# One attention routine: DVE's copy of transposed probabilities ahead of the newest maximum, transposes ahead of scores where there are three score buffers

## The reference, cut to what matters

```
s = jnp.einsum('bqhd,bkhd->bhqk', q_blk, k).astype(jnp.float32) * scale
p = jax.nn.softmax(s, axis=-1).astype(v.dtype)
return jnp.einsum('bhqk,bkhd->bqhd', p, v)
```

## The kernel before, in words

| prefix | what | key columns | loops x pairs of heads | score buffers |
|---|---|---|---|---|
| am | latent, layer one | 1024 | 2 x 2 | 3 |
| ad | dilated, layer one | 1024 | 2 x 2 | 3 |
| aa | maps, two later layers | 1280 | 2 x 2 | 2 |
| ab | grouped, two later layers | 1280 | 1 x 3 | 2 |
| ac | neighbourhood, two later layers | 256 or 384 near, 256 context | 1 x 3 | 3 |

## Time and profile before

### The profile page before, as it was taken

One profiled execution on the slowest core, in us unless ns is written; L12 is line 12 of the kernel. 1 busy time (PEld: TensorE's weight loads), 2 busy tenths in 40 slices (PEclk: granted clock), 3 DMA queues, 4 the chain that ended last, 5 costly groups with the idle time before them and its releaser, 6 DMA issues. The chain is left out here.

```text
span 4864.1 us, 71195 instructions
## 1 busy us (share of the span) xinstructions
PE 3732.1 (77%) x24823; PEld 3032.3 (62%) x24823; DVE 2448.6 (50%) x4501; ACT 2216.1 (46%) x3911; POOL 912.1 (19%) x749
## 2 busy tenths in 40 slices
PE   4497589788529999468997868765868997869657
PEld 3495377566428888357775657654657775658446
DVE  0303355343278788584443545555584444546564
ACT  0313455572127777432224656555332225657452
POOL 0021200000015665224460000000024450000002
PEclk7698799899659999779998999987989998989888
DMA  9334820421369999422222414152222223232333
GB/s 372 114 100 144 225 60 17 108 75 44 113 173 394 395 395 397 148 89 91 93 95 64 110 39 105 37 130 70 92 76 86 96 92 85 75 81 58 78 107 93
DMA packets 328051, 633.97 MB, mean 130 GB/s; under 512 B 115025, under 2 KB 171249, under 8 KB 326673
## 3 DMA queue, kind: packets, MB, share of 16 engines
q1 hardware_dynamic: 292220, 510.37, 33.4%
q0 software_dynamic: 33840, 113.66, 7.3%
q10 hardware_dynamic: 1636, 5.39, 0.3%
HBM read 490.39 MB, written 138.95 MB: 129 GB/s over the span
## 5 line engine op out<-in xcount | busy, mean ns | idle before, releaser
L1809 PE MATMUL pr_ps<-pr_wH,hT_part 128*128 128x512 f32 x1120 | 447.5, 400 | 0.0
L1579 ACT ACTIVATE ex_high<-ex_ring 128x2048 fp32r<-128x2048 f32 x192 | 368.6, 1920 | 95.6 <-PE ex_pg L1555 37.6
L1625 DVE TENSOR_TENSOR ex_ring_part<-ex_ring,ex_high 128x2048 fp32r<-128x2048 f32 x144 | 370.9, 2576 | 50.9 <-ACTq L1580 39.3
L1809 PE MATMUL pr_ps<-pr_wH,x_sb_part 128*128 128x512 f32 x896 | 366.7, 409 | 22.7 <-DVEq L1882 22.7
L1809 PE MATMUL pr_ps<-pr_w_part,x_sb_part 128*128 128x512 f32 x896 | 359.1, 401 | 0.0
L1116 DVE TENSOR_REDUCE aa_nm<-aa_ps 128x1 f32<-128x1280 f32 (+1 forms) x144 | 197.7, 1373 | 307.5 <-PE aa_ps L1030 306.7
L1520 POOL TENSOR_TENSOR ex_ring_part<-ex_ring,ex_high 128x2048 fp32r<-128x2048 f32 x48 | 238.6, 4971 | 215.0 <-ACTq L1580 215.0
L1040 PE MATMUL aa_ps<-ident,aa_prob 128*128 128x128 f32 x1312 | 209.7, 293 | 61.2 <-ACTq L1159 60.1
L1155 ACT ACTIVATE aa_prob<-aa_ps,aa_nm 128x512 f32<-128x512 f32 (+2 forms) x272 | 211.1, 776 | 88.4 <-DVEq L1117 44.5
L1809 PEld LDWEIGHTS pr_ps<-pr_wH,hT_part 128*128 128x128 f32 x1120 | 217.5, 194 | 47.9
L1116 DVE TENSOR_REDUCE ab_nm<-ab_ps 128x1 f32<-128x1280 f32 (+1 forms) x108 | 148.3, 1373 | 193.6 <-PE ab_ps L1030 193.2
(11 more groups left out here) (352 smaller groups left out, 9187.2 us busy)
## 6 DMA issues: line engine op xcount, KB each, us to landing
ex_ring<-in_w_gate SPq DMA_DIRECT2D x64, 1024.0 KB, 9.7
ex_ring<-in_w_up SPq DMA_DIRECT2D x64, 1024.0 KB, 8.3
ex_ring<-in_w_down SPq DMA_DIRECT2D x64, 1024.0 KB, 8.1
mod_w<-in_w_ada SPq DMA_DIRECT2D x24, 2048.0 KB, 12.8
z_d<-pr_zT POOLq DMA_DIRECT2D x120, 256.0 KB, 3.0
pr_w<-in_w_in SPq DMA_DIRECT2D x14, 2048.0 KB, 8.7
proj<-pr_raw POOLq DMA_DIRECT2D x60, 256.0 KB, 2.3
w_out<-in_w_out SPq DMA_DIRECT2D x3, 4096.0 KB, 18.8
```

Of the source, the lines that this page charges most:

```text
L1579: scalar.activation(wH[:, c % HL].bitcast(F32R), w_sb[:, c % SL], ACT.Copy)
L1625: vector.tensor_tensor(w_part[:, c % SL].bitcast(F32R), w_sb[:, c % SL], wH[:, c % HL], ALU.subtract)
L1809: mm = tensor.matmul(ps[:, g % 4, :], x.bitcast(F32R), w[:, c % 2, kk, :].bitcast(F32R), start=kk == 0 and i == 0, stop=kk == KC - 1 and i ...
```

## The change

On DVE the copy of g moves from the end of an iteration to its beginning, ahead of the normalization and of the maximum of h, for all stages. On TensorE, where LAG is 2 (three buffers), the transposes of g move ahead of the scores of h; where LAG is 1 the order stays. Where DVE has no part of the transposed columns (ad, context tiles) it no longer waits for the transposes, and TensorE no longer signals `tr`, so that `tr` is counted by steps that have such a part (`parts_before`).

```
+        def parts_before(g):
+            return sum(by_dve(t) is not None for _, t, _ in steps[:g])
...
                         if by_dve(t):
                             mm.then_inc(tr, 1)
-                        else:
-                            credit(pe, tr, 1)
...
                     for h in range(n + 4 + LAG):
                         g = h - LAG
-                        if h < n:
+                        if h < n and LAG == 1:
                             scores(h)
                         if 0 <= g < n:
                             transposes(g)
+                        if h < n and LAG == 2:
+                            scores(h)
...
                 def body(it):
+                    def turned_part(g):
+                        if 0 <= g < n:
+                            p, t, j = steps[g]
+                            if by_dve(t):
+                                dve.wait_ge(tr, it * parts_before(n) + parts_before(g + 1))
+                                cols = slice(*by_dve(t))
+                                vector.tensor_copy(pT[:, g // 2 % 2, j, cols], ps[g % SB][:, cols])
+                                dve.drain()
+                            credit(dve, evd, 1)
+
+
                     for h in range(n + 4 + LAG):
                         g = h - LAG
+                        turned_part(g)
                         if g % 2 and g >= 5:
...
                             dve.drain().then_inc(mx, 1)
-                        if 0 <= g < n:
-                            p, t, j = steps[g]
-                            dve.wait_ge(tr, it * n + (g + 1))
-                            if by_dve(t):
-                                cols = slice(*by_dve(t))
-                                vector.tensor_copy(pT[:, g // 2 % 2, j, cols], ps[g % SB][:, cols])
-                                dve.drain()
-                            credit(dve, evd, 1)
```

## The result

The changed kernel takes 5308.15 us (median of 4 runs, 5300.04 to 5312.23), the kernel before 4876.56 (4 runs): 432 us more, a ratio of 1.0886, interval 1.0869 to 1.0903. The forecast was slower, 5198, range 5140 to 5290. The direction was right and the size was not: of 432 us 323 were forecast, and the time lies above the range. It lies above 5150 to 5300 too, which is what the forecast's own bounds add up to.

What follows compares the result with a forecast made beforehand. The prediction took exponential, transposes and ScalarE's copy to bound two buffers, and mostly scores, maximum and DVE's copy three. 391 - 68 = +323 on 4865.8 made 5189, forecast as 5198 because the median lies 9 higher; range 5140 to 5290.

Steps and rivals of the forecast that it cites:

- two-buffer chain: aa, ab: maximum joins exponential, transposes, copy, every second step normalization too; a step costs 1.86 and 1.73 us more.
- total of 391: aa and ab: 227 us for 122 links, 159 for 92, and 5 for context tiles and their links.
- hand-over from maximum to exponential: aa, ab: time from DVE's maximum to ScalarE's exponential, taken as 0.2 us in aa and 0.1 in ab.
- context tiles and the links at them: 28 tiles of 256 columns without DVE copy, and links from and to them: +5 us together.
- rival 3: aa and ab: TensorE's granted clock falls, 143 us more, 5341 in all; chance 0.07.
- am: TensorE itself: am: TensorE's own work is late next, 3.48 us a step against 3.87, saving 23 us.
- the same step for ad and ac: What is late next: ScalarE in ad, 3.31 us against 3.44; DVE in ac, 2.65 against 3.10, saving 38.
- Two signs that the forecast gave: Trace after, am: scores start 3.5 us apart, and TensorE waits for no copy.
- Rival 2: am, ad, ac gain nothing: the maximum still waits for scores, and scores now for transposes; 5266 us, chance 0.10.
- Rival 1: DVE's slack absorbs the wait: two-buffer stages stay at 3.89 and 3.82, three-buffer ones gain; 4807 us, chance 0.04.
- Rival 4: Two buffers: the maximum might still be taken first, so no change; chance 0.01.
- term for the three-buffer stages: am, ad, ac: copy and maximum leave the row between two scores; -68 or -69 us, bounded by -80 and -20.

Runs made afterwards that it cites:

- e6: Two-buffer stages as changed, but DVE normalizes behind the maximum; three-buffer stages as in the kernel before: 5132.4 us against 4871.9.
- e2: The change in the three-buffer stages (am, ad, ac) alone, two-buffer stages as in the kernel before: 4920.64 us against 4871.05, ratio 1.0095.
- e3: Three-buffer stages with TensorE's transposes first but DVE in the old order; two-buffer stages as in the kernel before: 4894.02 us, ratio 1.0041.
- e7: Three-buffer stages as changed, output in two banks, its turn behind the next values' first half; two-buffer stages as before: 4817.79 us against 4871.9.
- e8: Three-buffer stages as changed, output in two banks, late turn, DVE's normalization behind the maximum; two-buffer stages as before: 4789.46 us, ratio 0.9828.
- e4: Three-buffer stages with DVE's copy first but TensorE's scores still ahead of transposes; two-buffer stages as before: 5045.12 us, ratio 1.0353.
- e10: Three-buffer stages with copy first, normalization last, output in two banks, but scores ahead of transposes; two-buffer stages as before: 4850.2 us against 4871.78.

## Why the prediction was right and where it failed

**The two-buffer chain was right.** The step that DVE's copy draws the maximum onto the chain of exponential, transposes, copy, maximum is what the rows of aa show, and e6 confirms its second part, the normalization. The total of 391 met 390.3 by luck, since four errors offset each other. The hand-over from maximum to exponential was taken 0.14 too long in aa (17 us) and 0.04 in ab (4). A normalization stands in 90 of the 214 links between full steps, not in 107 (19 us). Two errors went the other way. The context tiles and the links at them were put at 5 us and took some 14. And the clock fell: aa ran at a granted clock of 0.85 in both layers (0.94 and 0.96 before) and ab at 0.91 and 0.95 (0.99 before), where the forecast had charged nothing. Two windows of aa in the changed kernel, one long and one within a step, columns as in the earlier trace rows:

```profile
2612.00:2740.00 128.00, 91.83 (x678) 67.12 (x678) 49.56 (x84) 65.04 (x128) 0.98 (x1) 0.85 0.25 52
2693.00:2697.00 4.00, 2.58 (x15) 2.01 (x17) 0.49 (x2) 3.01 (x6) 0.00 (x0) 0.79 0.00 0
```

The timeline of the step in the second window shows what the lower clock does to the chain:

```profile
2695.08 1.35 PE L1043 MATMUL aa_ps<-ident,aa_prob 128*128 128x128 f32 x6 [0.44 <-ACTq L1166]
...
2696.46 0.42 DVE L1100 COPY aa_pT<-aa_ps 128x256 f32<-128x256 f32 x1 [3.39 <-PE aa_ps L1043]
```

From transposes to copy 1.38 us instead of 0.91, 0.47 for that step. Over all 122 links between full steps of aa the mean is 5.73. With 50 of them holding a normalization the undisturbed lengths have a mean of 5.50, so the links are about 28 us longer in sum, all but 2 us of it in links with a lower clock; in ab it is about 10 us. So rival 3 was there in part, for a quarter of its 143 us.

**The step that failed** is "am: TensorE itself", with the same step for ad and ac: what is late next once copy and maximum no longer stand in one row. I checked that the exponential is ready for its transposes, and did not check the turn, of which I had only counted the length. The small copy of the output is behind the exponential of the step before in ScalarE's queue, so everything that delays a maximum delays the turn, and TensorE's values and transposes stand behind the turn. The change moved both sides: the maximum came later on DVE by copy and, at odd steps, normalization, and the turn came earlier on TensorE by one block of transposes. In ad, which has no DVE copy, the second alone made it longer, by 3 us in the changed kernel and by 6 and 7 in e2 and e3, which have the same order there. So the forecast left out the loop of 7.99 us for two steps in am, where it had 2 x 3.48, and of 6.84 in ac, where it had 2 x 2.65. The term was mis-signed: -68 forecast, +46 in the trace, +50 in e2. Two signs that the forecast gave for the trace after did not show either: scores of am 3.5 us apart, and TensorE waiting for no copy; it waits for the small one.

**With that loop cut, the forecast's bounds come near.** e7 has DVE's order as forecast and the turn late: -54 for -68, am -20 for -23, ad -13 for -8, ac -21 for -38. In ac what is missing lies in the loop that e7 does not cut there; with the normalization last (e8) the steady steps of ac come to the forecast's 2.65 and ac gains 50. That is more than 38, which had been worked out with 88 links instead of the 92 of the trace; some 10 us of the gain were not traced.

**Rival 2** (three-buffer stages gain nothing, 5266) was nearest of all on these stages, with the wrong mechanism: it blamed scores for being late behind transposes. Alone, transposes first do cost 23 us (e3), but DVE's half costs more without them (e4), and with the turn out of the way they are worth 60 (e8 against e10). In total rival 3's 5341 is nearer to 5308, by luck: the clock took a quarter of what it charged, and the loss in three buffers did the rest. **Rival 1** (DVE's slack absorbs the wait) was wrong: the changed kernel is the slower, and the three-buffer stages did not even show the gain in it. Nor do shares single out TensorE: it is the fullest by matmuls, 114.30 us of 130, but by weight loads it has 87.06 and ScalarE 93.93. **Rival 4** did not occur.

**The range was too narrow** because its term for the three-buffer stages, -80 to -20, excluded a loss without a row for it. The bound was on the size of a gain whose sign rested on one unchecked queue.

## What to carry to other kernels

When an instruction is moved, follow each engine's queue around a full period, small operations included, until it comes back to itself: a copy of 0.28 us behind an exponential closed a loop of 8 us. An engine whose queue is short on work is still a place in the chain if it takes things in order: put first what others wait for soonest, and what is waited for latest (here the normalization) last. And split a change by family before believing its sum; here one half cost 390 us, and the other half's idea was worth 82 once turn and normalization were out of its way.

## What the runs showed of the hardware

The granted clock of TensorE went with its waits: in ac 0.98 and 0.96 in e8, 0.92 and 0.94 before, 0.85 and 0.88 in the changed kernel, 0.76 and 0.77 in e4, in the order of the stages' lengths. No run changed the waits and kept the rest, so this is a parallel and not a proof. What such a stretch costs can be read: in e4 a block of six score matmuls, in a stretch with a mean granted clock of 0.62 behind a wait of the turn for 2.12 us, took 2.42 us, and in the steady state of before 1.63.
